# The mixer's last dense layer as four pairs of seven half-size products

## What is computed

```
proj = h @ w_in                                  # h = rmsnorm(x, g_mix)
...                                              # ya: differential attention, yb: forget attention
merged = jax.nn.sigmoid(ga) * (ya @ w_diff_out) + jax.nn.sigmoid(gb) * (yb @ w_fox_out)
x = x + merged @ w_o                             # the layer that is changed
x = x + _memory_cross_attention(_rmsnorm(x, g_mem_q), ...)
```

## Time and profile before

| | |
|---|---|
| Median of 3 runs | 2421.91 us (2419.7 to 2423.41) |
| Profiled execution | 2418.93 us, of it the span of the trace 2417.1 us |
| TensorE busy | 2380.2 us, 98% of the span |
| VectorE, GpSimd, ScalarE busy | 60%, 40%, 39% |
| Stage `w_o`, first multiplication to the next stage's first | 1449.04 to 1536.08 us |

### The profile page before, as it was taken

How to read it: one execution, slowest core, us unless ns; L and a number is a source line. 1 busy time by engine, 2 the same in 40 slices (tenths; PEclk the granted TensorE clock), 3 DMA queues, 4 the chain that set the end, 5 groups by cost and what they waited for, 6 DMA issues and landing times. The chain is left out here.

```text
span 2417.1 us, 33874 instructions
## 1 busy us (share of the span) xinstructions
PE 2380.2 (98%) x12098; PEld 1991.6 (82%) x12098; DVE 1452.3 (60%) x2353; ACT 949.9 (39%) x1767; POOL 977.3 (40%) x779
## 2 busy tenths in 40 slices
PE   9999999999999999999999999999999999999998
PEld 5888888887888888888888888887877888888886
DVE  5856565566455446445554653445586666798878
ACT  5443434343134334434444521334243333444443
POOL 1313131322572222232212233311366666798786
PEclk9999999999999999999999999999999999999999
DMA  8413130314452222122122245211315544644442
GB/s 362 133 71 90 54 113 27 109 51 156 139 187 75 84 71 74 45 84 79 44 74 79 95 135 185 85 44 44 104 42 154 171 149 148 235 168 155 149 149 87
DMA packets 86393, 271.94 MB, mean 113 GB/s; under 512 B 9176, under 2 KB 9304, under 8 KB 81120
## 3 DMA queue, kind: packets, MB, share of 16 engines
q1 hardware_dynamic: 63664, 184.37, 22.9%
q10 hardware_dynamic: 22576, 85.61, 11.0%
HBM read 198.08 MB, written 58.23 MB: 106 GB/s over the span
## 5 line engine op out<-in xcount | busy, mean ns | idle before, releaser
L750 POOL CAST w_hi<-raw 128x1024 fp32r<-128x1024 f32 x112 | 120.5, 1076 | 1066.7 <-issue 369.7
L3090 PE MATMUL ps<-act_hi,w_hi 128*128 128x512 f32 x1248 | 499.0, 400 | 1.9 <-DVE act_lo L2681 1.1
L3092 PE MATMUL ps<-act_hi,w_lo 128*128 128x512 f32 x1248 | 488.5, 391 | 0.0
L3091 PE MATMUL ps<-act_lo,w_hi 128*128 128x512 f32 x1248 | 486.7, 390 | 0.0
L752 POOL TENSOR_TENSOR w_lo<-raw,w_hi 128x1024 fp32r<-128x1024 f32 x112 | 277.1, 2474 | 9.0
L3092 PEld LDWEIGHTS ps<-act_hi,w_lo 128*128 128x128 f32 x1248 | 234.2, 188 | 51.9
L3090 PEld LDWEIGHTS ps<-act_hi,w_hi 128*128 128x128 f32 x1248 | 234.6, 188 | 45.1 <-DVE act_lo L2681 1.5
L3091 PEld LDWEIGHTS ps<-act_lo,w_hi 128*128 128x128 f32 x1248 | 234.9, 188 | 40.6
L3106 PE MATMUL ps<-act_hi,w_hi 128*128 128x512 f32 x384 | 150.5, 392 | 2.4 <-POOL w_lo L752 1.2
L3108 PE MATMUL ps<-act_lo,w_hi 128*128 128x512 f32 x384 | 149.6, 390 | 0.0
L3110 PE MATMUL ps<-act_hi,w_lo 128*128 128x512 f32 x384 | 118.3, 389 | 0.0
(11 more groups left out here) (554 smaller groups left out, 5817.7 us busy)
## 6 DMA issues: line engine op xcount, KB each, us to landing
raw<-in_w_stream_dram SPq DMA_DIRECT2D x192, 512.0 KB, 3.7
x_own_f<-a_dram SPq DMA_DIRECT2D x32, 512.0 KB, 5.4
a_dram<-stage SPq DMA_DIRECT2D x18, 512.0 KB, 6.3
ada<-in_w_ada_dram SPq DMA_DIRECT2D x4, 2048.0 KB, 23.9
spill<-res ACTq DMA_DIRECT2D x16, 512.0 KB, 5.0
gate_dram<-gate_sb ACTq DMA_DIRECT2D x32, 256.0 KB, 2.0
stage<-spill ACTq DMA_DIRECT2D x16, 512.0 KB, 4.2
act_lo_f<-a_dram SPq DMA_DIRECT2D x16, 512.0 KB, 5.5
```

What stands on the lines that cost most here:

```text
L750: nc.gpsimd.tensor_copy(w_hi[:, s, :, :], raw[:, s, :, :]).then_inc(S["w_hi"], 1)
L3090: nc.tensor.matmul(out, wh, xh, start=start, stop=False, skip_group_check=onto)
L3091: nc.tensor.matmul(out, wh, xl, start=False, stop=False, skip_group_check=onto)
L3092: return nc.tensor.matmul(out, wl, xh, start=False, stop=stop, skip_group_check=onto)
```

## The change

The layer `w_o` is computed two output rows at a time (a "pair" or block n of four), each by seven products of half size (512 x 512 activation parts with 256 x 512 weight parts) instead of eight. The quarters of the pair's weights are a11, a12, a21, a22 (`raw`, output tile o, half h of the inputs), those of `merged` are rows 0 to 3 and 4 to 7, left and right half of the tokens. Products 1, 4 and 5 take weight quarters as they are, products 0, 2, 3 and 6 take sums of quarters; products 1, 4 and 6 take parts of `merged` as they are, products 0, 2, 3 and 5 take sums of its parts. Every operand has a high and a low part again. The order on TensorE is 1, 0, 4, 6, 3, 2, 5. Products 4, 6 and 5 are added onto banks that hold 1, 0 and 3, so each waits until that bank has been read: 4 for ScalarE's copy of product 1 (`first_copied`), 6 for VectorE's read of product 0, 5 for VectorE's read of product 3.

GpSimd makes the four weight sums and seven low parts of each pair (`block_weights`), ScalarE the high parts (`block_high`). The sums of the parts of `merged` are made by VectorE inside the merge's rows; their low parts by GpSimd for the sum of product 0 (`t_lo`) and by VectorE for the other three (`t_low_part`). The two raw tiles of a pair are released together, by the last low part of the pair. VectorE puts the products together (`block_sums`). The sum of squares moves behind the whole first tile of the query projection, and the loads of the memory's keys and values behind the layer.

```diff
+        LP_ORDER = (1, 0, 4, 6, 3, 2, 5)
+        LP_CHUNK = {1: 0, 0: 1, 4: 2, 6: 3}
...
+        def lp_place(n, i, act, w, own):
+            if i in LP_CHUNK:
+                return act[:, LP_CHUNK[i], BANK:T]
+            return own if i == 5 else quarter(w, n % 2, 0 if i == 3 else 1)
...
+        T_HIGHS = ([(0, j) for j in range(4)] + [(3, 0), (3, 1), (3, 2), (2, 0), (3, 3), (2, 1), (2, 2), (2, 3)]
+                   + [(5, j) for j in range(4)])
...
+        def lp_x(lp, i, k):
+            if i in T_SET:
+                return (T_HI, T_LO)[lp][i][k]
+            row, h = {1: (k, 0), 4: (k + 4, 0), 6: (k + 4, 1)}[i]
+            return (act_hi, act_lo)[lp][:, row, h * BANK:(h + 1) * BANK]
...
+            def t_lo(i, j):
+                pool.wait_ge(S["lt_hi"], lt_count("lt_hi", T_HIGHS, i, j))
+                nc.gpsimd.tensor_tensor(T_LO[i][j], T_WHOLE[i][j], T_HI[i][j].bitcast(F), ALU.subtract
+                                        ).then_inc(S["lt_lo"], 1)
+            for t in range(2, 8):
+                split((T_MERGE + t) // 2, t % 2)
+                if 3 <= t < 7:
+                    t_lo(0, t - 3)
...
+            def block_weights(n):
...
+                def low(i, whole):
+                    pool.wait_ge(S["lw_hi"], lw_high_count(n, i))
+                    nc.gpsimd.tensor_tensor(lp_lo(n, i), whole, lp_hi(n, i).bitcast(F), ALU.subtract
+                                            ).then_inc(S["w_split" if i == (5 if n else 2) else "lw_lo"],
+                                                       2 if i == (5 if n else 2) else 1)
...
+                pool.sem_inc(S["w_hi"], 2)
+                loaded(0)
+                if n == 0:
+                    low(1, a11)
+                    low(4, a12)
+                    loaded(1)
+                    low(5, a22)
+                else:
+                    loaded(1)
+                    summed(3, s3, a21, a11, ALU.subtract)
+                    low(1, a11)
+                summed(0, s1, a21, a22, ALU.add)
+                sum_made(0)
+                summed(2, s2, s1, a11, ALU.subtract)
+                if n:
+                    low(0, s1)
+                    low(4, a12)
+                sum_made(2)
...
+                if n == 0:
+                    summed(3, s3, a21, a11, ALU.subtract)
+                    low(0, s1)
+                low(6, late)
+                low(3, s3)
+                low(2, s2)
+                if n:
+                    low(5, a22)
+            for n in range(4):
+                block_weights(n)
+            pool.wait_ge(S["lp_done"], lp_done(2, 2))
+            split(T_MQ // 2, 0, free=False)
+            pool.wait_ge(S["tile_done"], T_WO + 7)
+            split(T_MQ // 2, 1, free=False)
...
+            def block_high(n, i):
+                if i in (1, 4, 5):
+                    act.wait_ge(S[f"raw_in{i // 5}"], 16 * (T_WO // 2 + n) + 16)
+                else:
+                    act.wait_ge(S["lw_sum"], lw_sum_count(n, i))
+                if n and i in LP_CHUNK or n and i == 5:
+                    act.wait_ge(S["lp_done"], lp_done(n - 1, i))
+                nc.scalar.activation(lp_hi(n, i), lw_whole(n, i), ACT.Copy).then_inc(S["lw_hi"], 1)
...
+            def first_copied(n):
+                if n >= 2:
+                    act.wait_ge(S["lin_evac"], WO_ROWS + 2 * (n - 1))
+                act.wait_ge(S["lp_done"], lp_done(n, 1))
+                nc.scalar.activation(first_part[:, n % 2, :], lp_bank(n, 1), ACT.Copy).then_inc(S["lp_copied"], 1)
...
+            for i in (1, 4, 5, 0):
+                block_high(0, i)
             sigmoids(1, 6)
             merged_hi(0, 6)
+            for i in (2, 6, 3):
+                block_high(0, i)
+            act.wait_ge(S["spilled"], 128)
+            act.wait_ge(S["tile_done"], T_WO)
+            x1_load(0)
+            act.wait_ge(S["lo_ready"], 8 * FILL["merged"] + 7)
+            for i, j in T_HIGHS[4:8]:
+                t_hi(i, j)
+            first_copied(0)
             merged_hi(1, 6)
...
-            pairs_in(0)
-            pairs_in(1)
...
+            for n in range(4):
+                if n:
+                    first_copied(n)
+                    for s in range(2):
+                        residual_square("wo", "x2", s, n - 1)
+                        residual_kept("wo", s, n - 1)
+                if n:
+                    block_high(n, 5)
+                if n < 3:
+                    for i in (3, 1, 0):
+                        block_high(n + 1, i)
+                    if n:
+                        x1_load(n + 1)
+                    for i in (2, 4, 6):
+                        block_high(n + 1, i)
+            for k in range(KT):
...
+                    act.wait_ge(S["lp_done"], lp_done(3, LP_ORDER[k]))
+                act.wait_ge(S["lin_evac"], WO_ROWS + k + 1)
                 gained_hi("x2", k)
-            act.wait_ge(S["tile_done"], T_WO + 8)
-            gained_hi("x2", 4)
-            gained_hi("x2", 5)
+            residual_square("wo", "x2", 0, 3)
             residual_square("wo", "x2", 1, 3)
             residual_kept("wo", 0, 3)
...
+            act.wait_ge(S["tile_done"], T_WO + 8)
...
+                dve.wait_ge(S["mg_step"], 3 * row + 9)
+                if row < 4:
+                    t_sum(0, T_WHOLE[0][j], left, right, ALU.subtract)
+                    low()
+                else:
+                    dve.wait_ge(S["lt_sum"], lt_count("lt_sum", T_SUMS, 0, j))
+                    t_sum(2, T_WHOLE[2][j], right, T_WHOLE[0][j], ALU.add)
+                    if row >= 6:
+                        low()
+                    if row < 7:
+                        last_sums(row)
+                    if row < 6:
+                        low()
...
+                for i, x in ((3, T_WHOLE[3][j]), (5, left)):
+                    nc.vector.tensor_tensor(T_WHOLE[i][j], x, T_WHOLE[2][j], ALU.subtract).then_inc(S["lt_sum"], 1)
...
+                    nc.vector.tensor_tensor(out, x, y, op).then_inc(S["lp_ev"], 1)
...
+                read(0, 1, add[:, 1, right], add[:, 1, right], lp_bank(n, 0), ALU.subtract)
+                if n != 1:
+                    dve.wait_ge(S["lt_lo"], LEFT["lt_lo"] + (4, 0, 8, 12)[n])
+                read(4, 2, res[:, a, left], add[:, 0, left], lp_bank(n, 4), ALU.add)
+                read(6, 3, res[:, a, right], add[:, 0, right], lp_bank(n, 6), ALU.subtract)
+                dve.wait_ge(S["lp_ev"], LEFT["lp_ev"] + 5 * n + 1)
+                read(3, 4, add[:, 1, right], add[:, 1, right], lp_bank(n, 3), ALU.add)
+                dve.wait_ge(S["lp_copied"], LEFT["lp_copied"] + n + 1)
+                read(2, 5, part, part, lp_bank(n, 2), ALU.add)
+                dve.wait_ge(S["lp_ev"], LEFT["lp_ev"] + 5 * n + 5)
+                nc.vector.tensor_tensor(res[:, a, right], res[:, a, right], part, ALU.add).then_inc(S["lin_evac"], 1)
+                nc.vector.tensor_tensor(add[:, 1, left], add[:, 1, left], part, ALU.add).then_inc(S["lp_part"], 1)
+                nc.vector.tensor_tensor(res[:, b, right], add[:, 1, right], part, ALU.add).then_inc(S["lp_part"], 1)
+                dve.wait_ge(S["lp_part"], LEFT["lp_part"] + 2 * n + 2)
+                if n < 3:
+                    dve.wait_ge(S["lp_done"], lp_done(n, 5))
+                else:
+                    dve.wait_ge(S["tile_done"], T_WO + 8)
+                nc.vector.tensor_tensor(res[:, b, left], add[:, 1, left], lp_bank(n, 5), ALU.add
+                                        ).then_inc(S["lin_evac"], 1)
...
+            last_sums(7)
+            t_lows(3, range(3))
+            block_sums(0, {1: [lambda: t_lows(3, [3])], 2: [lambda: t_lows(2)], 3: [lambda: t_lows(5)]})
             nc.vector.memset(acc2[:, :], 0.0)
             dve.drain()
-            residual_gained("wo", T_WO, "x2")
+            for n in range(1, 3):
+                block_sums(n, {2: [lambda s=s, n=n: add_square("wo", "x2", s, n - 1) for s in range(2)]})
+            block_sums(3, {1: [lambda: gained_lo("x2", 0)],
+                           2: [lambda: gained_lo("x2", 1)] + [lambda s=s: add_square("wo", "x2", s, 2) for s in range(2)],
+                           3: [lambda: gained_lo("x2", 2)],
+                           4: [lambda: gained_lo("x2", 3)]})
+            for k in range(4, KT):
+                gained_lo("x2", k)
+            add_square("wo", "x2", 0, 3)
+            add_square("wo", "x2", 1, 3)
...
-            pe.wait_ge(S["lo_ready"], 8 * FILL["merged"] + 7)
-            with pe.Fori(0, 3) as i:
-                linear_pair("wo", T_WO, "merged", i)
-            linear_pair("wo", T_WO, "merged", 3, last=True)
...
+            def block_product(n, i):
...
+                out, onto = lp_bank(n, i), i >= 4
+                if i == 1:
+                    if n < 2:
+                        pe.wait_ge(S["mg_step"], 26 + 3 * n)
+                    else:
+                        pe.wait_ge(S["lin_evac"], WO_ROWS + 2 * (n - 1))
+                if i == 4:
```

(22 more changed lines are left out.)

198 lines of the change are left out of this document (157 added, 41 removed).

## The result

The changed kernel has a median of 2430.22 us (2428.13 to 2430.85, 5 runs), beside 2419.7 us for the kernel before on the same chip: a ratio of 1.0039, 95% interval 1.0029 to 1.005 (it is taken over the single runs; the two medians alone give 1.0043). The forecast was 2431.0 us and +0.38%. Its profiled execution took 2430.85 us.

What follows compares the result with a forecast made beforehand. TensorE's multiplications and its few waits were taken as the bound: -10.9 - 0.4 + 3.6 + 3.5 + 5.4 + 4.1 + 3.0 + 0.8 = +9.1 us, giving a median of 2431.0 us (+0.38%), range 2418 to 2438 us.

Steps and rivals of the forecast that it cites:

- Removed work: TensorE in the changed layer: 384 multiplications become 336, 48 fewer at 0.2267 us each, -10.9 us.
- The next stage's -0.4: Stage after the layer: its 0.42 us wait for a low part can go or stay; counted as -0.4 us.
- The last merged row: Product 4 of block 0: ScalarE's queue delays row 7's low part, TensorE waits 3.6 us; bounds 0.8 and 5.
- The burst: Block 0: VectorE's sums and low parts delay its reads; product 6 waits 3.5 us, product 5 5.4 us.
- The prices: Two-input 512-column instructions: VectorE 0.62 us alone, 1.75 beside GpSimd's two-input work, the engines taking turns; GpSimd 1.25 alone.
- the rival without contention: Whole kernel: VectorE and GpSimd do not hinder each other in this stage; -7 us, 2415 us; chance 0.12.
- The ring: Raw tiles, GpSimd: 20.8 or 22.3 us a pair against TensorE's 19.0; waits of 4.1 us in blocks 2 and 3.
- VectorE in block 3: Low parts and additions of squares queued between VectorE's reads: product 5 waits 3.0 us; bounds 0.5 and 4.
- The clock: Half clock after TensorE's waits, four of them over 2.04 us: +0.8 us in all, partly hidden in next waits; bounds 0 and 5.
- One of the signs that I named: Changed profile: TensorE's waits in this stage come to 15 to 22 us.
- as I had named it: Sign in the changed profile: VectorE's 512-column low parts have a median near 1.7 us where GpSimd works.
- It comes out even: Rival: start on time, burst stands, 9.8 us of waits, -1.5 us, within 4.8 us of 2421.9; chance 0.22.

Runs made afterwards that it cites:

- experiment 1: Changed kernel with ScalarE doing the gate's sigmoid and row 6's high part before the fourth high part of block 0's weights: median 2426.12 us.
- 5: Changed kernel with 14 filler multiplications on TensorE before product 4's wait for row 7's low part in block 0: median 2429.62 us.
- 7: Changed kernel with GpSimd held from block 1's weights until VectorE has read product 3 of block 0: median 2433.9 us.
- 8: Changed kernel with a pair's first raw tile released by product 4's low part, and GpSimd's and ScalarE's orders moved to suit: median 2420.61 us.
- 2: Changed kernel with ScalarE making product 5's high part before the copy of product 1 and the previous pair's squares: median 2427.12 us.
- 11: The tenth plus GpSimd held from block 1's weights until VectorE's last low part of block 0: median 2415.02 us, ratio 0.9976 to the kernel before.
- 6: Changed kernel with VectorE reading product 0 of block 0 ahead of the last two sums and product 3's four low parts: median 2433.24 us.
- 4: Changed kernel with 18 filler multiplications on TensorE before product 5's wait in block 0: median 2430.25 us.
- 3: Changed kernel with VectorE's 12 subtractions for low parts replaced by one-input copies: median 2426.48 us.
- the tenth: Changed kernel with the edits of experiment 1, 2, 6 and 8 together, block 3's order left as in the changed kernel: median 2420.55 us.

## Why the prediction was right

- **Removed work.** -10.9 us: 48 multiplications, at the same spacing. The next stage's -0.4 was -0.7.
- **The last merged row.** 3.6 us forecast, 3.49 measured, for the reason given, ScalarE's order: experiment 1 takes 2.6 of it away. Row 7's multiplications start at 1454.18 where I had 1453.4, with the layer itself 0.9 us later.
- **The burst.** Forecast: 3.5 and 5.4 us; measured 1.77 and 4.59. The places were right to half a us (product 6 resumed 15.2 us after the layer's start, forecast 15.2; product 5 28.3, forecast 28.8), so VectorE's queue was followed rightly. At product 6 most of the difference is half clock, which I had put into the clock's term with the right remark that it shortens the next wait (5). At product 5 it is VectorE's read, which came half a us early, and TensorE's slower starts.
- **The prices.** 1.75 us for a two-input instruction of VectorE beside GpSimd, 0.62 alone: 5.77 for four, as one alone and three in turns would take (estimate, 0.62 + 3 x 1.75 = 5.9), and 2.49 for four with GpSimd held (7). The rival without contention, 2415 us, fell with that. The turns are no law: in 1 and 8 GpSimd's instruction waited through the rest of VectorE's burst.
- **The ring.** 22.2 us measured (GpSimd's first instructions of blocks 2 and 3 are 1496.62 and 1518.80), 22.3 forecast; waits 3.2 us, forecast 4.1. What I had not seen is ScalarE's part in block 1, worth 2.6 us in blocks 2 and 3 (2).
- **VectorE in block 3.** 3.0 forecast, 1.74 measured; with the 1.7 us of half clock ahead of it, 3.4.
- **The clock.** The term that was mis-sized: +0.8 forecast, 6.0 measured, beyond the 5 that I had as a bound. 3.1 of them (behind product 4 of blocks 0 and 3) only filled time in which VectorE was not ready, and were missing in the waits that follow (shown for block 0 by 5, argued for block 3); 2.9, behind product 5 of block 0, were a loss of their own in the layer, for TensorE waits for no other engine in block 1. Two readings under this term were off as well: five of the forecast waits, not four, are longer than 2.04 us, and the six multiplications behind that wait took 1.4 us longer by their starts, not 1.7.

By terms, then: 20.4 us of losses in the layer were forecast, 22.8 came. Two errors cancelled: the waits came to 14.8 us where 19.6 were forecast, the clock and the slower restarts to 8.0 where 0.8 was. The profiled span grew by 12.0, where 9.1 was forecast; 0.9 of it lies ahead of the layer. The medians, 10.5 us apart, stand between. That the forecast of 2431.0 us missed by only 0.8 is luck in part: it stood on 2421.91 us for the kernel before, whose median beside the changed one was 2419.7. One of the signs that I named was off: the waits sum to 14.8 us, just under my 15. Of VectorE's twelve low parts the seven that had to wait for GpSimd have a median of 1.77 us, as I had named it; the mean of all twelve is 1.27, since the other five took 0.68.

One rival was near. "It comes out even" is the changed kernel with edit 8 (2420.61 us), but not by the start being on time, which still waited 3.50 us. And the direction of the change was not a matter of the work itself: with five orders changed (11), the same instructions of VectorE, ScalarE and GpSimd and 336 multiplications are 5 us faster than before.

## What to carry to other kernels

When one engine sets the time and a change takes work from it, write the other engines' queues out in order and in time, at the prices they have beside each other: here 10.9 us of saved multiplications stood against 22.8 us of waits and half clock, at six places that an order of instructions decided. A buffer of two slots should be released slot by slot by its last reader, and not at the end of the group of work: with the reordering that this needs it was worth 9.7 us, some 6.6 of them behind block 0. A burst of VectorE's SBUF work should be put where GpSimd rests, since each instruction of GpSimd between two of VectorE's costs it 1.1 us (1.75 against 0.62). Holding GpSimd for it gained only where its ring was short enough: 4.6 us in 11, but nothing in the median in 7. And a wait that is filled or moved is won only if the next one is for another cause (5, 6).

## What the runs showed of the hardware

- VectorE's one-input cast of 128x512 from SBUF to SBUF takes 0.36 us alone and 1.38 beside GpSimd, whose instructions then take 1.36 to 1.47; VectorE's two-input ones take 0.62 and up to 1.75. I had expected the cast to be free of it. The Trainium skill (SBUF — State Buffer, section SBUF: two separate sides) has the pair of ports as an exclusive lock for a whole instruction, taken by VectorE's two-port modes as well as by its instructions with two SBUF inputs; by that rule, the trace agrees in both forms (1.38 us against 0.36, 1.75 against 0.62). With VectorE's burst under way it was GpSimd's instruction that took 2.95 us (1) and 2.80 (8), where it takes 1.25 alone. VectorE's reads of PSUM beside the same work stayed at 0.67 to 0.69 us.
- Half clock stood behind TensorE's waits of 3.49, 4.59 and 2.47 us in the changed kernel, where it cost 1.4 to 2.9 us each time, and soon behind 2.15 us in the eighth; not behind 1.77 in the changed kernel and 1.61 in the eleventh. The length of the wait alone does not decide: 2.46 us before product 4 of block 3 had full clock behind it in 4 and half clock in 3 and 6, and 2.99 us in 2 had full clock. In the tenth it stood behind the sum of squares (16 multiplications with one column), with no wait at all, in the eleventh the same sum was followed by full clock. What decides between these two is left open.
